# Level differences of a gated linear attention: four half-width subtractions become two full-width ones, and the exponential takes the sign

## The reference

```python
q, k, v, r, z_f, z_b = jnp.split(proj, ...)          # proj = h @ w_in
log_g = -softplus(-(z @ w_g2 + b_g)) / TAU           # TAU = 16, one gate per head, channel and token
b = jnp.cumsum(log_g, axis=2)
rel = where(causal, b[:, :, :, None] - b[:, :, None, :], -inf)
scores = einsum('bnihd,bnjhd,bnijhd->bnhij', q, k, exp(rel))
o_intra = einsum('bnhij,bnjhv->bnihv', scores, v)
```

## Time and profile before

| what | before |
|---|---|
| median of 3 runs | 1563.86 us (1563.14 to 1564.26) |
| profiled execution, its own time | 1566.78 us |
| profiled execution, span | 1565.1 us |
| PE busy | 1521.6 us, 97% |
| DVE busy | 1136.7 us, 73% |
| ACT busy | 658.5 us, 42% |
| POOL busy | 184.7 us, 12% |
| mean granted clock of PE | 0.991 |

### The profile page before, as it was taken

The page is one execution under the profiler, slowest core; times in us unless marked ns, Lnnn a source line. Parts: engine busy times, 40 slices in busy tenths (PEclk is TensorE's granted clock), DMA queues, the critical chain, the costliest instruction groups (busy, mean ns, idle before and its releaser), DMA issues.

```text
span 1565.1 us, 24633 instructions
## 1 busy us (share of the span) xinstructions
PE 1521.6 (97%) x8788; PEld 1501.6 (96%) x8788; DVE 1136.7 (73%) x1728; ACT 658.5 (42%) x942; POOL 184.7 (12%) x278
## 2 busy tenths in 40 slices
PE   7999999999979999999999999999989999999998
PEld 7999999999979999999999999998779999999998
DVE  6898888878996877779887777986977574444432
ACT  3433342259975433332343333224546454333321
POOL 0010000100250000001100000100795000000000
PEclk9999999999989999999999999999999999999999
DMA  9466676622433555667545556753222134334421
GB/s 359 179 242 226 211 250 207 221 74 95 141 101 121 194 194 182 198 223 242 190 160 190 187 189 226 236 195 111 73 76 88 61 108 139 129 122 140 155 93 40
DMA packets 68918, 257.03 MB, mean 164 GB/s; under 512 B 7648, under 2 KB 9696, under 8 KB 68608
## 3 DMA queue, kind: packets, MB, share of 16 engines
q1 hardware_dynamic: 49664, 188.03, 35.3%
q0 software_dynamic: 18432, 67.12, 12.9%
q10 hardware_dynamic: 768, 1.19, 0.2%
HBM read 253.68 MB, written 2.63 MB: 164 GB/s over the span
## 4 chain that ended last, share of the span: by engine, by line
PE 88%; DVE 5%; ACT 3%; POOL 2%; issue 1%; DMA 0%; SPq 0%; DVEq 0%; ACTq 0%; POOLq 0%
PE bank L536 25%; PE bank L538 25%; PE bank L537 25%; PE bank L642 2%; PE bank L589 1%; PE bank L590 1%; PE bank L593 1%; PE bank L549 1%; ACT w_hi_sb L916 1%; PE wide L769 1%; DVE w_lo_sb L1344 1%; DMA ada_first<-in_ada_w 0%; PE bank L791 0%; DVE bcum L1858 0%; DVE h_lo L1430 0%
## 5 line engine op out<-in xcount | busy, mean ns | idle before, releaser
L916 ACT ACTIVATE w_hi_sb<-raw 128x1024 fp32r<-128x1024 f32 (+3 forms) x308 | 344.0, 1122 | 483.3 <-PE bank L538 456.8
L536 PE MATMUL bank<-h_hi,w_hi_sb 128*128 128x384 f32 x1570 | 530.4, 338 | 2.3 <-ACT vt L1314 1.0
L1344 DVE TENSOR_TENSOR w_lo_sb<-raw,w_hi_sb 128x1024 fp32r<-128x1024 f32 (+3 forms) x308 | 403.1, 1310 | 175.3 <-ACT w_hi_sb L916 172.7
L537 PE MATMUL bank<-h_lo,w_hi_sb 128*128 128x384 f32 x1570 | 528.0, 336 | 0.0
L538 PE MATMUL bank<-h_hi,w_lo_sb 128*128 128x384 f32 x1570 | 527.9, 336 | 0.0
L536 PEld LDWEIGHTS bank<-h_hi,w_hi_sb 128*128 128x128 f32 x1570 | 295.6, 188 | 6.4 <-DVE h_lo L1430 2.1
L537 PEld LDWEIGHTS bank<-h_lo,w_hi_sb 128*128 128x128 f32 x1570 | 295.5, 188 | 0.0
L538 PEld LDWEIGHTS bank<-h_hi,w_lo_sb 128*128 128x128 f32 x1570 | 295.4, 188 | 0.0
L536 PE MATMUL bank<-a_hi,w_hi_sb 128*128 128x384 f32 x704 | 236.9, 336 | 1.4 <-DVE a_lo L1493 1.4
L537 PE MATMUL bank<-a_lo,w_hi_sb 128*128 128x384 f32 x704 | 236.6, 336 | 0.0
L538 PE MATMUL bank<-a_hi,w_lo_sb 128*128 128x384 f32 x704 | 236.6, 336 | 0.0
(11 more groups left out here) (286 smaller groups left out, 1663.9 us busy)
## 6 DMA issues: line engine op xcount, KB each, us to landing
raw<-in_ffn_in SPq DMA_DIRECT2D x176, 512.0 KB, 3.6
ada_raw<-in_ada_w POOLq DMA_DIRECT2D x128, 512.0 KB, 3.6
raw<-in_ffn_out SPq DMA_DIRECT2D x64, 704.0 KB, 4.2
raw<-in_rg_in SPq DMA_DIRECT2D x20, 512.0 KB, 3.5
ada_first<-in_ada_w SPq DMA_DIRECT2D x8, 1024.0 KB, 14.2
raw<-in_rg_out SPq DMA_DIRECT2D x8, 640.0 KB, 3.8
raw<-in_gla_qk SPq DMA_DIRECT2D x8, 512.0 KB, 3.3
raw<-in_gla_v SPq DMA_DIRECT2D x8, 512.0 KB, 3.4
```

The costliest lines, as they stand in the source:

```text
L536: pe.matmul(out, w_hi_sb[:, slot, w], hi[k], start=start and j == 0, stop=False)
L537: pe.matmul(out, w_hi_sb[:, slot, w], lo[k], start=False, stop=False)
L916: A(w_hi_sb[:, s, 0:w], raw[:, s, 0:w], ACT.Copy).then_inc(w_hi, 1)
L1344: V.tensor_tensor(w_lo_sb[:, s, 0:w], raw[:, s, 0:w], w_hi_sb[:, s, 0:w].bitcast(F32), ALU.subtract).then_inc(w_split, 1)
```

## The change

POOL makes two subtractions of 128 x 384 for each level, one per direction, b - ref over both halves of a block, into one of two new slots `d_slot[k % 2]` (in unused columns of `w_lo_sb`). ACT turns them into the factors with four exponentials of 128 x 192, two with scale 1/TAU and two with -1/TAU, and writes `e_slot[k % 4]`. The wait for the slot of level k - 4 moves from POOL to ACT. POOL waits instead, from k = 2 on, until the exponentials of k - 2 are done. Step 0 has two levels in place of three; after it the counts alternate the other way (2, 3, 2, 3, ... in place of 3, 2, 3, 2, ...), so that step 7 has three in place of two, and from step 8 on nothing differs. The exponentials of the levels of step 0 (now one, k = 0) are issued after the last q/k block, where before k = 0 came one block earlier.

```diff
-        w_lo_sb = sb("w_lo_sb", [P, RING, WMAX], F32R)
+        w_lo_scope = ExitStack()
+        w_lo_sb = sb("w_lo_sb", [P, RING, WMAX], F32R, w_lo_scope)
+        w_lo_scope.close()
+        d_store = sb("d_store", [P, RING, WMAX])
...
-        for count in (3, 2, 3, 2, 3, 2, 3, 2, 2, 2, 2, 2, 2, 2, 0, 0, 0):
+        for count in (2, 3, 2, 3, 2, 3, 2, 3, 2, 2, 2, 2, 2, 2, 0, 0, 0):
...
+        d_slot = [d_store[:, 2 * j:2 * j + 2, DC * P:WMAX] for j in range(2)]
...
-                    if n >= 4:
-
-                        pn = n - 4
-                        pool.wait_ge(s_done, pn // NLEV * (NLEV + 1) + pn % NLEV + 2)
-                    f, b = (bcum[:, hd, j, :].rearrange("p (n h s) -> p n h s", h=2, s=s) for j in range(2))
-                    eq, ek = (e_slot[n % 4][:, j, :].rearrange("p (n h s) -> p n h s", h=2, s=s) for j in range(2))
+                    if n >= 2:
+                        pool.wait_ge(e_ready, n - 1)
                     nb = T // (2 * s)
-                    ref_f = f[:, :, 0, s - 1:s].to_broadcast([P, nb, s])
-                    ref_b = b[:, :, 1, 0:1].to_broadcast([P, nb, s])
-                    nc.gpsimd.tensor_tensor(eq[:, :, 1, :], f[:, :, 1, :], ref_f, ALU.subtract)
-                    nc.gpsimd.tensor_tensor(eq[:, :, 0, :], b[:, :, 0, :], ref_b, ALU.subtract)
-                    nc.gpsimd.tensor_tensor(ek[:, :, 0, :], ref_f, f[:, :, 0, :], ALU.subtract)
-                    nc.gpsimd.tensor_tensor(ek[:, :, 1, :], ref_b, b[:, :, 1, :], ALU.subtract).then_inc(d_ready, 1)
+                    for j in range(2):
+                        b = bcum[:, hd, j, :].rearrange("p (n h s) -> p n h s", h=2, s=s)
+                        ref = (b[:, :, 0, s - 1:s] if j == 0 else b[:, :, 1, 0:1]).to_broadcast([P, nb, 2 * s])
+                        last = nc.gpsimd.tensor_tensor(d_slot[n % 2][:, j, :].rearrange("p (n u) -> p n u", u=2 * s),
+                                                       bcum[:, hd, j, :].rearrange("p (n u) -> p n u", u=2 * s),
+                                                       ref, ALU.subtract)
+                    last.then_inc(d_ready, 1)
...
-                    A(e_slot[k % 4], e_slot[k % 4], ACT.Exp, scale=1.0 / TAU).then_inc(e_ready, 1)
+                    if k >= 4:
+                        pn = k - 4
+                        act.wait_ge(s_done, pn // NLEV * (NLEV + 1) + pn % NLEV + 2)
+                    w = LEVELS[l - 1]
+                    f, b = (d_slot[k % 2][:, j, :].rearrange("p (n h s) -> p n h s", h=2, s=w) for j in range(2))
+                    eq, ek = (e_slot[k % 4][:, j, :].rearrange("p (n h s) -> p n h s", h=2, s=w) for j in range(2))
+                    A(eq[:, :, 1, :], f[:, :, 1, :], ACT.Exp, scale=1.0 / TAU)
+                    A(ek[:, :, 0, :], f[:, :, 0, :], ACT.Exp, scale=-1.0 / TAU)
+                    A(eq[:, :, 0, :], b[:, :, 0, :], ACT.Exp, scale=1.0 / TAU)
+                    A(ek[:, :, 1, :], b[:, :, 1, :], ACT.Exp, scale=-1.0 / TAU).then_inc(e_ready, 1)
...
-                if b >= DC - 2:
-                    level_exp(LEVELS_AT[0][b - DC + 3])
+                if b == DC - 1:
+                    for n in LEVELS_AT[0]:
+                        level_exp(n)
```

## The result

The change makes the kernel slower: a median of 1572.21 us (six runs, 1569.35 to 1575.63) against 1563.95 us of the kernel before on the same chip (six runs, 1563.14 to 1564.71). The medians are 8.3 us apart; the ratio, which is taken over all runs, is 1.0048 [1.0037, 1.0059], or 7.5 us (5.8 to 9.2). The forecast was 1571, 7.2 us more, with its own range 1567.5 to 1575. The profiled execution took 1575.1 us, span 1573.4; the one of before 1566.8 and 1565.1.

What follows compares the result with a forecast made beforehand. The prediction took PE, busy 97% of the span, as the bound. First keys 1.0, steps 1, 3 and 5 2.7, step 7 2.5, r stage 1.0 and clock 0 sum to 7.2 us: 1563.9 + 7.2 = 1571 us, range 1562 to 1579.

Steps and rivals of the forecast that it cites:

- Steps 1, 3 and 5: Value stage: PE waits 1.75 us before each third level, replacing gaps of 2.54 and 0.61; +2.7 us in sum.
- Step 7: Its third level needs merge 17, behind three value copies on DVE; 4.4 us to the first r block, +2.5.
- First keys: DVE's keys before the first keyed level come 1.0 us later, bounds -0.5 to +2.
- r stage: ACT pays 0.27 us more for each of nine levels, 2.4 if all exposed; taken as +1.0 us.
- The hold of a wide subtraction: A DVE operation meeting a 128 x 384 POOL subtraction waits 0.75 us, bounds 0.62 and 0.83; 0.3 for a narrow one.
- POOL's part: POOL's two wide subtractions take 1.8 us a level (1.7 to 2.0) against 1.87 before: its own work the same within 0.1.
- the third head's round: On DVE before the first keys: POOL waits for the exponentials of k = 0, so this round is undisturbed, 1.5 us better.
- POOL's extra lateness: Steps 1, 3 and 5: POOL, no longer four slots ahead, waits for exponentials of k - 2; 0.6 us added once (0 to 5).
- Clock: PE's half clock behind long gaps: one stretch goes, another may follow step 7's gap; taken as 0 (-1.6 to +3.2 us).
- Rival 1: POOL ahead of all: wide subtractions hold DVE no longer than about 0.4 us, kernel faster, 1560 to 1562 us; chance 0.13.
- Rival 3: POOL becomes the bound in the value stage, PE gaps of 2.5 to 3.5 us with half clock, +14: 1578 us; chance 0.18.

Runs made afterwards that it cites:

- e2: The changed kernel with four POOL subtractions of 128 x 192 per level in place of two of 128 x 384: 1570.20 us, ratio to the kernel before 1.0036.
- e3: The changed kernel with DVE's three value copies in step 7 moved behind merges 17 and 18: 1570.72 us, ratio to the kernel before 1.0041.
- e1: The changed kernel with the old step counts and the first exponentials where they were: 1567.01 us, ratio to the kernel before 1.0018.
- e9: The changed kernel with four difference slots, POOL waiting for the exponentials of k - 4 instead of k - 2: 1573.72 us, ratio to the kernel before 1.0057.
- e10: The changed kernel with narrow subtractions (128 x 192), old step counts and the first exponentials where they were: 1568.42 us, ratio to the kernel before 1.0032.
- e11: The kernel before with new counts, later k = 0 exponential, value copies behind merges 17 and 18, small scalings and last low weights behind first keys: 1565.00 us, ratio 1.0003.
- e4: The kernel before with only the new step counts and the later exponential of k = 0: 1566.32 us, ratio to the kernel before 1.0012.
- e8: The changed kernel with old counts and early exponentials, DVE's small scalings and last q/k block's low weights behind the first keys: 1567.98 us, ratio to before 1.0015.
- e5: The changed kernel with only DVE's five small scalings moved behind step 0: 1573.53 us, ratio to the kernel before 1.0053.
- e7: The kernel before with DVE's small scalings and the last q/k block's low weights moved behind the first keys: 1564.76 us, ratio to the kernel before 1.0001.
- e12: The kernel before, unedited, run once more for a second profile: 1563.64 us (one run).
- e6: The changed kernel with one exponential of 128 x 768 per level, sign left out, in place of four of 128 x 192: 1570.01 us, ratio to before 1.0044.

## Why the prediction was right

The time, the sign and the mechanism held: DVE's chain meets longer holds, three levels in steps 1, 3 and 5 are paid in gaps ended by merges, and step 7 waits behind its copies. The sum of the terms was 7.2 and the stage shows 7.28. That this is within 0.1 is luck: first keys and r stage came out dearer by 1.0 and 1.1 us, the time from the first keys to step 7 cheaper by about 2.2 (0.45 measured, clock included, where +2.7 was forecast).

- **The hold of a wide subtraction: 0.75 taken, 0.62 to 0.67 measured**, near the lower bound. Keys 1.58 against 0.94 alone, weights 1.80 to 1.88 against 1.19, a scan pair 2.41 against 1.79. The `y_lo` row that it leaned on the earlier trace rows writes another kind of tile and is slower alone (1.02 against 0.82). The rule of the Trainium skill ("SBUF — State Buffer", section "SBUF: two separate sides") that the lock is held for a whole instruction goes with it: 0.65 for 384 columns, 0.3 for 192. DVE operations that read PSUM show no dependence on the width: the three copies of values took 1.87 beside wide subtractions and 1.89 beside the narrow ones of before, the merges 0.58 in both.
- **POOL's part: 1.8 us a level forecast, 1.64 alone.** The shortest took 0.82 us each. That is 0.23 less than the 1.87 of before, where 0.07 was forecast. With the waits, the 28 levels took 72.4 us, and 88.9 both in e2 and in the kernel before: of the 16.5 us that the width won POOL, 6.4 are its own work and 10 come from meeting DVE less often.
- **First keys: +1.0 forecast, +2.04 measured**, just over its upper bound of 2. From the first gate operation to the one of the third head +0.29 (0.6 forecast); the third head's round -1.47 (-1.5); from the last head's first operation to the first keys +3.22, where 1.5 was forecast for the scan and the weights and 0.4 for the keys. Scan and weights measured 1.23 and the keys that PE waits for met nothing; the five small scalings, which the prediction didn't count, went from 0.36 us to 2.35. That is the term that was mis-sized: the list of DVE operations that can meet POOL left them out.
- **Steps 1, 3 and 5: gaps of 1.75 forecast, 0.62, 1.50 and 1.52 measured.** With a hold of 0.65 the forecast's own chain gives 1.55. The first is short since PE itself was late behind its half clock. POOL's extra lateness (0.6) did not show. In sum 3.64 in place of 3.15, +0.5, where +2.7 was forecast; what the clock took ahead of the first is in neither. This term has the largest error of the sum, 2.2 us.
- **Step 7: 4.4 us from the end of the last value part to the first r block forecast, 4.51 measured** (1171.38 to 1175.89), +2.66 for +2.5. e3 shows that the copies are its cause.
- **r stage: +1.0 forecast, +2.13 measured.** Not from exposed exponentials as such: 0.73 is the gap before head 2's outputs, and about 1.2 the half clock behind step 7's gap. In e1, where no half clock reaches into the r stage, it is +1.0.
- **Clock: 0 forecast.** Half clock was 3.2 and 3.2 us before, and 5.75 and 3.4 now, so 1.4 us more lost: within its range. Part of it is hidden in the shorter first of the three gaps.

Rival 1 needed holds under 0.5 us and fell with them. Rival 3 needed POOL to be the bound with wide subtractions; e9 excludes it: without any wait for POOL the gaps stay. Only kernels with narrow subtractions show a gap of PE behind a wait for POOL (e10, e11). What the prediction does not say is that the counts and the width do not add: undoing the counts gives 4.7 us with wide subtractions (5.5 of the stage) and 0.6 with narrow ones (e2 against e10; 2.5 of the stage), and adding them costs the kernel before about 2 (e4). The two gains differ by 4.1 us with an uncertainty of some 3.5.

What stays open is the last 2.8 us of e1. In its profile the first keys are 2.4 us later than before and the r stage is 1.0 longer, and 1.65 is won between, where it has one stretch of half clock less. It has the four exponentials, the moved waits and the wide holds before the first keys, whose gap of 5.58 is by far its largest; e8 took that gap away and did not become faster, in a profile with 10 us of half clock. The runs don't part these, and none tests whether it matters that the differences now lie in another tile than the factors.

## What to carry to other kernels

Where an engine shares a lock with the one that is behind, count its operations by how long each keeps the other out, not by their sum, and put into the list every small operation of the chain too: five of them that need half a microsecond alone cost two here. Wider instructions let the one engine through sooner (2.6 against 3.2 us a level) and hold the other longer at each meeting (0.65 against 0.3), so they pay only where the first one is late. A buffer that lets an engine run ahead can cost time for the same reason (e9). An edit of the order on an engine that is behind can move a gap without closing it (e5, e7, e8); it helps where the work that is put off is not what is waited for next (e3). Ask which gap comes next before taking a shorter one for a gain.

## What was not expected of the hardware

- The same idle time of PE is not always followed by the same clock. In the kernel before, a gap of 2.75 us ahead of the same level was followed by 1.2 GHz once (0.61 in the window of the earlier trace rows) and by 2.4 GHz the other time (e12). Gaps of 3.81 (e10) and 2.96 (e6) kept the full clock, one of 2.18 (e8) lost it. In e7 the level behind a gap of 2.77 ran at full speed, and the clock fell 1.25 us after its start. Once down, it stayed down for 3 to 6 us where PE went on working (5.75 behind the gap of 5.21), and for some 10 us in e8, with a gap of 1.73 within. The six runs of the changed kernel lie 6 us apart, and the two slowest have the lowest mean clock (0.989, the two fastest 0.993 and 0.994), so the clock likely has the larger part in this. The kernel before spread over 1.6 us beside it and over 5.3 us in another batch (23 runs).
- A scaling of 128x4 floats from one SBUF tile to another waits for POOL as long as a product of 128x768 does: 0.155 us alone, up to 0.84 beside the wide subtraction, and `spare` (128x8) 0.48 beside the narrow one against 0.16. The page cited above names operations with two SBUF inputs or in a two-port mode, and counts `tensor_scalar` among those that can enter such a mode; these have one input, and no run here shows in which mode they run.
- On POOL, subtractions of 192 columns are issued 0.47 us apart, and one of 384 takes 0.82 alone: one wide in place of two narrow ones saves 0.12 us.
